# A Hyena filter in the middle of a transformer kernel: decays spread earlier, spectra without the norm, the norm put into the short convolution's weights

## The chip, the cores and the metric

The kernel runs on one core of one Trainium2 chip. The metric is the device time of one execution in microseconds (us). A core has five engines that run their own instruction streams and meet in semaphores: TensorE (PE in the profile; PEld is its weight load), VectorE (DVE), ScalarE (ACT), GpSimd (POOL) and SyncE (SP, which here only issues transfers). SBUF is the on-chip memory of 128 partitions, PSUM holds eight banks of 128 x 512 f32 for the results of matmuls.

## The reference, cut to what matters

The program is a whole model on 512 tokens of width 1024: a first block (a mixer of three attentions, a memory attention, a feed-forward with a convolution), and a second block with four feed-forwards, one pool/Hyena mixer and one latent attention. The change touches the Hyena mixer's filter and what surrounds it:

```python
h = jnp.sin(sin_freq[0] * (z @ w1 + b1))     # three such layers, z: (512, 33), hidden 64
h = (h @ w_out).reshape(L, HYENA_ORDER, 2, HYENA_WIDTH)          # (512, 2, 2, 512)
h = h * jnp.exp(-t[:, None, None, None] * jnp.abs(decay))
fwd, bwd = h[:, :, 0], h[:, :, 1]
two = jnp.concatenate([fwd, zeros, bwd[:0:-1]], axis=0)           # length 1024
two = two * lax.rsqrt(jnp.sum(two * two, axis=0, keepdims=True))
spec = jnp.fft.rfft(two, axis=0)
# in the mixer, for o in 0, 1:
y = irfft(rfft(u, n=2 * L) * spec[o])[:L];  y = y + u * bias[o];  z = parts[o] * y
```

`parts` are the three outputs of a short convolution of width 3 (weights `hyena_conv_w`, bias `hyena_conv_b`) over a projection. The result of the filter does not depend on the tokens.

## The kernel before, in words

**Weights.** All large projections read weights in packs of 128 x 1024 f32 (512 KB). SP loads pack n into one of two raw buffers (L660 to L666) once POOL has split pack n-2. ACT rounds the pack to its high part (`split_high`, L1388), three packs ahead of their use; POOL subtracts to get the low part (`split_low`, L714); PE does three matmuls for each 128 x 128 tile (high x high, high x low, low x high; `pack`, L752, its lines L763 to L765). Four slots of high and low parts are in use. Eight tiles make a pack of a projection, 22 tiles in three packs make one output of a down projection.

**Order of the work.** Each engine has its stream written out by hand. PE: the feed-forward `conv` (L1082), filter layer 1, the feed-forward `ffn0` (L1084), then the filter stage, then the projection `pool_hyena` (16 packs, L1139), then the mixer with its transforms, its out projection and the rest of the second block. In a feed-forward PE does 44 packs up, one small matmul for the filter's hidden layer (`filter_layer`, L1066), and 24 packs down. After pack 0 of the next projection PE sums the squares for the norm (`stats`, L768); ACT takes a root (`root`, L1415), DVE the reciprocal (`norm`, L1983). For each output of a down projection DVE adds the residual and prepares a chunk of the next input (`chunk`, L1965 on DVE, L1401 on ACT). After `conv` the norm is a double one: DVE also accumulates `gained_sq` (L1981, L2354), which the statistics at L775 wait for.

**The filter stage** begins when the last output of `ffn0` has been added to x.
1. ACT issues six transfers on its own queue: the cosine and sine tables (L1759 to L1765), and makes `neg_times` (L1769). PE spreads the four decay rows over the partitions, a matmul of a column of ones with one row each (L1091, banks 4 to 7), and makes the filter of time tile 0 (L1099, banks 0 to 3). ACT takes the absolute value of the spread decays (L1772), then the exponentials for time tile 0 (L1778).
2. For the four time tiles t: DVE multiplies filter and decay (L2369), adds and subtracts the two directions into `fsum` and `fdiff` (L2376, L2377). ACT squares (L1790). PE makes the filters of t+1 and sums the squares of t with a matrix of ones (L1116). In place of filters of a fifth tile PE does the middle row (four matmuls with the alternating signs, L1110).
3. PE makes the spectra in four groups g = (half of the frequencies, order), each eight f32 matmuls into four banks: cosine even, cosine odd, sine even, sine odd (L1134). Group g+2 uses the banks of group g, and waits for `spec_taken`.
4. ACT makes `inv_norm` (Ln, Exp with -0.5, L1799, L1801) and scales the bias row, which a transfer has broadcast to all partitions (L1797, L1803). DVE, for each half group, multiplies even by `inv_norm`, adds the bias to the cosines, multiplies odd by `inv_norm`, adds and subtracts both into `spec` (L2406 to L2413). After groups 0 and 1 it works on the middle row, one partition wide (`middle`, L2388 to L2398).
5. PE starts `pool_hyena` pack 0 when six of the eight half groups are taken (L1138), its statistics wait for all eight (L1143). ACT splits pack 3 (L1807 with j = 0) ahead of this, right after the bias.

Of the kernel before, what the change touches and what calls it, by code (L numbers as in the profile page):

```python
# [26 lines left out]
P = 128  # L27
# [172 lines left out]
def build_program(nc, A, out):  # L200
# [158 lines left out]
    absdecay = put("absdecay", [P, 4 * T])  # L359
# [4 lines left out]
    decay_row = nc.alloc_sbuf_tensor_at("decay_row", [P, T], F32, offset=m3f + 4096)  # L364
# [3 lines left out]
    put, m4n = region(window_at)  # L368
    inv_norm = put("inv_norm", [P, 2, T])
    waves_tmp = put("waves_tmp", [P, 2, T])  # L370
    bias_b = put("bias_b", [P, 2, T])
    assert m4n["at"] <= window_at + 4128 + 2048 + 8192
# [56 lines left out]
    STAT = 7  # L429

# [89 lines left out]
    bias_b_arrived = sem("bias_b_arrived")  # L520
# [16 lines left out]
    norm_read = sem("norm_read")  # L537
    norm_ready = sem("norm_ready")
    bias_scaled = sem("bias_scaled")
# [104 lines left out]
    def _(sp):  # L644
# [22 lines left out]

        load_x(0)
# [76 lines left out]
    def _(pe):  # L745
# [46 lines left out]
        def project_out(phase, rhs, ready, packs_each=1, total=8, order=None):  # L792

            with pe.Fori(0, 2) as i:
                for j in range(4):
                    wait_bank(phase, i, 4, j)
                    for c in range(packs_each):
# [277 lines left out]

        def feed_forward(name, s, hidden_base, layer=None):
            project(name + "_up", 2 * FC, LIN, (chunk_ready, 8 * s), s=s)
            if layer is not None:
                filter_layer(layer)
            project_out(name + "_down", (act_hi, act_lo), (hidden_low, hidden_base), packs_each=3, total=FC)  # L1080
# [6 lines left out]
        pe.wait_ge(wout_arrived, 16 * 6)  # L1087
# [15 lines left out]
        for t in range(QT):  # L1103
            if t + 1 < QT:
                filters(t + 1)
            else:
                pe.wait_ge(fsum_ready, 2)
                for o in range(2):
                    for u in range(2):
                        mm = pe.matmul(ps[0:1, 6 + o, :], col("nyquist"), fsum[:, u, o, :], start=(u == 0), stop=(u == 1))  # L1110
                mm.then_inc(mid_made, 1)
# [10 lines left out]
        for g in range(4):  # L1122
            ft, o = g // 2, g % 2
            cut = slice(ft * P, (ft + 1) * P)
            if g == 1:
                pe.wait_ge(norm_read, 1)
                pe.wait_ge(mid_read, 1)
            for part in range(4):
# [1616 lines left out]
```

## Time and profile before

| what | value |
|---|---|
| median of 3 runs | 2823.34 us (2818.3 to 2825.89) |
| the profiled execution, its own time | 2817.33 us |
| its span, first to last instruction | 2815.3 us |
| PE busy | 2743.7 us, 97% |
| DVE, ACT, POOL busy | 1171.4, 1029.2, 1113.1 us (42%, 37%, 40%) |
| mean granted TensorE clock | 0.995 |
| filter stage in the trace | about 1206 to 1278 us of the span |

Times in the trace are in us from the start of the span. A busy time of PE includes matmuls that overlap in its pipeline, so the spacing of their starts is what one costs. An idle time that the profile shows before an instruction is followed by the instruction of another engine that ended it. An f32 matmul of 512 columns is recorded as two instructions. Lines such as L1981 are lines of the kernel; a row of the timeline merges neighbours of one kind and says with x how many.

### The profile page before, as it was taken

The page shows a single profiled execution, that of the slowest core. Times are in us where ns is not written, and L with a number is a line of the kernel's source. Part 1 is how long each engine was busy: PE and PEld are TensorE (multiplying, and loading weights), DVE is VectorE, ACT ScalarE, POOL GpSimd, SP SyncE. Part 2 cuts the span into 40 slices and gives each one's busy share as a digit, 9 for nine tenths or more (in the row PEclk, how much of TensorE's full clock was granted, in tenths as well). Part 3 has the DMA queues.
Part 4 walks back from the last instruction along what each step waited for, and adds up shares of the span by engine and source line. Part 5 has one row for each costly group of instructions (what it writes and reads, how often), then busy time and mean ns, then how long its engine had stood idle before and what let it go on. Part 6 is the DMA issues. An engine that isn't in the chain of part 4 may idle for free.

```text
span 2815.3 us, 35415 instructions
## 1 busy us (share of the span) xinstructions
PE 2743.7 (97%) x12394; PEld 2174.1 (77%) x12394; DVE 1171.4 (42%) x1912; ACT 1029.2 (37%) x1571; POOL 1113.1 (40%) x473
## 2 busy tenths in 40 slices
PE   8999999999999999989999999999999989999998
PEld 6777777888887888847778888888888744788887
DVE  4886534645434225157873222122221356422212
ACT  4455433444333222242223222232322556323221
POOL 3334433444544444513224444444444420444443
PEclk9999999999999999999999999999999999999999
DMA  5333322333332333322113333333233210233332
GB/s 168 115 97 119 98 75 68 99 91 102 98 111 90 97 97 99 110 68 86 45 38 105 98 96 99 110 94 101 91 101 107 90 45 1 81 99 92 102 99 89
DMA packets 78106, 258.18 MB, mean 92 GB/s; under 512 B 8951, under 2 KB 14583, under 8 KB 77768
## 3 DMA queue, kind: packets, MB, share of 16 engines
q1 hardware_dynamic: 70848, 243.30, 28.3%
q10 hardware_dynamic: 7176, 13.78, 1.5%
q8 instruction: 52, 0.85, 0.1%
q14 instruction: 30, 0.25, 0.0%
HBM read 251.02 MB, written 6.03 MB: 91 GB/s over the span
## 4 chain that ended last, share of the span: by engine, by line
PE 92%; DVE 5%; ACT 1%; issue 1%; DMA 0%; ACTq 0%; DVEq 0%
PE ps L763 27%; PE ps L765 27%; PE ps L764 27%; PE ps L1301 1%; PE ps L1315 1%; PE ps L1329 1%; PE ps L1307 1%; PE ps L1116 1%; PE ps L1048 1%; PE ps L1058 0%; PE ps L981 0%; PE ps L982 0%; PE ps L983 0%; PE ps L883 0%; PE ps L966 0%
## 5 line engine op out<-in xcount | busy, mean ns | idle before, releaser
L716 POOL TENSOR_TENSOR wlo<-raw,whi 128x1024 fp32r<-128x1024 f32 x449 | 1099.1, 2451 | 1656.5 <-ACT whi L1393 1631.5
L763 PE MATMUL ps<-lin_hi,whi 128*128 128x512 f32 x2208 | 867.4, 393 | 6.6 <-DVE waves_tmp L2410 6.6
L765 PE MATMUL ps<-lin_hi,wlo 128*128 128x512 f32 x2208 | 860.2, 390 | 0.0
L764 PE MATMUL ps<-lin_lo,whi 128*128 128x512 f32 x2208 | 860.2, 390 | 0.0
L1393 ACT ACTIVATE whi<-raw 128x1024 fp32r<-128x1024 f32 x452 | 473.5, 1053 | 508.8 <-PE ps L765 443.0
L763 PEld LDWEIGHTS ps<-lin_hi,whi 128*128 128x128 f32 x2208 | 415.2, 188 | 98.9 <-DVE waves_tmp L2410 7.4
L764 PEld LDWEIGHTS ps<-lin_lo,whi 128*128 128x128 f32 x2208 | 415.2, 188 | 88.3 <-issue 2.6
L765 PEld LDWEIGHTS ps<-lin_hi,wlo 128*128 128x128 f32 x2208 | 415.1, 188 | 87.0
L763 PE MATMUL ps<-act_hi,whi 128*128 128x512 f32 x858 | 334.0, 389 | 0.0
L765 PE MATMUL ps<-act_hi,wlo 128*128 128x512 f32 x858 | 333.8, 389 | 0.0
L764 PE MATMUL ps<-act_lo,whi 128*128 128x512 f32 x858 | 333.8, 389 | 0.0
L2048 DVE TENSOR_TENSOR up<-ps,rstd 128x512 f32<-128x512 f32 x88 | 60.8, 691 | 395.4 <-PE ps L765 395.4
L1504 ACT ACTIVATE act_hi<-hidden 128x512 f32 (+1 forms) x88 | 55.6, 632 | 462.5 <-DVE hidden L2071 462.5
L1999 DVE SCALAR_TENSOR_TENSOR x<-ps,x 128x512 f32 x64 | 44.3, 692 | 375.0 <-PE ps L765 374.7
L763 PEld LDWEIGHTS ps<-act_hi,whi 128*128 128x128 f32 x858 | 161.1, 188 | 35.1 <-POOL wlo L716 0.8
L764 PEld LDWEIGHTS ps<-act_lo,whi 128*128 128x128 f32 x858 | 161.1, 188 | 33.6
L765 PEld LDWEIGHTS ps<-act_hi,wlo 128*128 128x128 f32 x858 | 161.1, 188 | 33.1
L2048 DVE TENSOR_TENSOR gate<-ps,rstd 128x512 f32<-128x512 f32 x88 | 60.8, 691 | 188.9 <-PE ps L765 188.2
L1408 ACT ACTIVATE scratch<-x 128x512 f32 x64 | 40.5, 633 | 229.6 <-DVE x L1999 229.6
L763 PE MATMUL ps<-o_hi,whi 128*128 128x512 f32 x256 | 100.5, 392 | 1.7 <-DVE o_lo L2592 1.7
L765 PE MATMUL ps<-o_hi,wlo 128*128 128x512 f32 x256 | 99.6, 389 | 0.0
L764 PE MATMUL ps<-o_lo,whi 128*128 128x512 f32 x256 | 99.6, 389 | 0.0
(374 smaller groups left out, 2704.3 us busy)
## 6 DMA issues: line engine op xcount, KB each, us to landing
raw<-in_packs SPq DMA_DIRECT2D x456, 512.0 KB, 3.6
table<-bias_scratch ACTq DMA_DIRECT2D x12, 256.0 KB, 3.0
bias_scratch<-biasrow ACTq DMA_DIRECT2D x16, 160.0 KB
x<-in_x_t SPq DMA_DIRECT2D x4, 512.0 KB, 8.3
out_t<-x SPq DMA_DIRECT2D x16, 128.0 KB, 1.8
bias_scratch<-biasrow ACTq DMA_DIRECT2D x4, 320.0 KB
mem<-in_mem_t ACTq DMA_DIRECT2D x1, 1024.0 KB, 5.5
pool_count<-in_pool_count ACTq DMA_DIRECT2D x1, 1024.0 KB, 4.9
```

Source lines behind the costliest of these rows:

```text
L716: pool.tensor_tensor(wlo[:, n % 4, :], raw[:, n % 2, :], whi[:, n % 4, :].bitcast(F32), ALU.subtract).then_inc(low_split, 1)
L763: pe.matmul(target, wh, hi[:, k, :], start=(chunk0 + at == 0), stop=False)
L764: pe.matmul(target, wh, lo[:, k, :], start=False, stop=False)
L765: mm = pe.matmul(target, wl, hi[:, k, :], start=False, stop=(chunk0 + at == total - 1))
L1048: mm = pe.matmul(ps[:, att2.banks(u)[0], 0:M], mem_q[:, 2 * h + c, qt * P:(qt + 1) * P], mem_k[:, 2 * h + c, :], start=(c == 0), stop=(c = ...
L1116: pe.matmul(ps[:, 4 + c // 2, :], ones[:, :], filt_sq[t % 2][:, c * T:(c + 1) * T], start=(t == 0 and c % 2 == 0), stop=(t == QT - 1 and c ...
L1301: mm = pe.matmul(ps[:, 2 * p + h, :], q_nope[r:r + 64, 2 * g + p, cut], k_nope[r:r + 64, 2 * g + p, :], start=True, stop=False)
L1393: act.activation(whi[:, n % 4, :], raw[:, n % 2, :], ACT.Copy).then_inc(high_split, 1)
L1408: act.activation(squares[:, d % 2, :], x[:, row, :].rearrange("p a t -> p (a t)"), ACT.Square).then_inc(squares_ready, 1)
L1504: act.activation(act_hi[:, bass.ds(f, 1), :].rearrange("p a t -> p (a t)"), h_buf, ACT.Copy).then_inc(hidden_high, 1)
L1999: dve.scalar_tensor_tensor(out=xc, in0=ps[:, j, :], scalar=factor, in1=xc, op0=ALU.mult, op1=ALU.add).then_inc(outs_done, 1)
L2048: dve.tensor_tensor(target, ps[:, 2 * g + side, :], rstd[:, :], ALU.mult).then_inc(outs_done, 1)
```

## The change

In words: the decay rows are loaded before `ffn0` (into the buffer of the position features, after filter layer 0 has read it), and `neg_times` is made there. The four spreading matmuls run between the up and down halves of `ffn0`, into banks 5, 6, 7 and 2, ACT takes the absolute values there; the third output of the down half waits for them. The six tables are loaded by SP, behind the load of `pool_hyena` pack 4. The middle row's matmuls move from the last square step to after spectrum group 0. The spectra are no longer scaled. The bias becomes an impulse at time 0 of `fsum`: the root of the sum of squares on one partition (ACT, Sqrt) times the bias (one small load), added to one row of `fsum`. The sums of squares, which every partition holds, are brought into columns by eight multiply-and-accumulate instructions with the identity, go through Ln and Exp as 128 x 8, and scale the weights and biases of the short convolution for the two gates. ACT copies each odd spectrum from PSUM, DVE does one add and one subtract for each half group; both middle rows come after group 1. ACT's split of pack 3 of `pool_hyena` comes after the copies.

The pieces follow the file: buffers, SP, PE, ACT, DVE.

```diff
-    absdecay = put("absdecay", [P, 4 * T])
-    decay_row = nc.alloc_sbuf_tensor_at("decay_row", [P, T], F32, offset=m3f + 4096)
+    decay_row = nc.alloc_sbuf_tensor_at("decay_row", [P, T], F32, offset=zpos_at)
+    absdecay = nc.alloc_sbuf_tensor_at("absdecay", [P, 4 * T], F32, offset=m3f + 4096)
+    filter_sums, inv_norm = small[:, 24:32], small[:, 32:40]
+    odd_waves = nc.alloc_sbuf_tensor_at("odd_waves", [P, 2, T], F32, offset=window_at)
+    DECAY_BANKS = (5, 6, 7, 2)
+    WAVE_ORDER = ((1, 0), (1, 1), (0, 1), (0, 0))
...
+        def load_waves():
+            sp.wait_ge(outs_done, OUT_BASE["pool_hyena"])
+            for wave, name in ((cos_f, "dcos"), (sin_f, "dsin")):
+                for half in range(2):
+                    src = A[name].rearrange("(p a) (u h) f -> h p a u f", a=2, h=2)[half][:, :, :, 0:256]
+                    sp.dma_start(wave[64 * half:64 * (half + 1), :, :].rearrange("p (a u) f -> p a u f", a=2), src).then_inc(waves_arrived, 16)
+            for wave, name in ((cos_i, "dcos"), (sin_i, "dsin")):
+                sp.dma_start(wave[:, :, :], A[name][:, 0:2, :]).then_inc(inverse_waves_arrived, 16)
...
             load(n, None)
+            if n == hyena + 4:
+                load_waves()
...
+        def spread_decays():
+            pe.wait_ge(decay_arrived, 16 * 4)
+            pe.wait_ge(final_rooted, 1)
+            pe.wait_ge(root_ready, 4)
+            pe.wait_ge(outs_done, OUT_BASE["ffn0_up"] + 2 * FC - 1)
+            for c in range(4):
+                pe.matmul(ps[:, DECAY_BANKS[c], :], ones[32 * c:32 * c + 1, :], decay_row[32 * c:32 * c + 1, :],
+                          start=True, stop=True).then_inc(decay_spread, 1)
...
-        for c in range(4):
-            pe.matmul(ps[:, 4 + c, :], ones[32 * c:32 * c + 1, :], decay_row[32 * c:32 * c + 1, :], start=True, stop=True).then_inc(decay_spread, 1)
...
             if g == 1:
-                pe.wait_ge(norm_read, 1)
-                pe.wait_ge(mid_read, 1)
+                for n in range(2):
+                    for u in range(2):
+                        mm = pe.matmul(ps[0:1, 6 + n, :], col("nyquist"), fsum[:, u, n, :], start=(u == 0), stop=(u == 1))
+                mm.then_inc(mid_made, 1)
+                pe.wait_ge(filter_steps, 2)
+                pe.wait_ge(roots_made, 1)
+            for at, (sines, odd) in enumerate(WAVE_ORDER):
+                wave, source = ((cos_f, fsum), (sin_f, fdiff))[sines]
+                if g == 1 and at == 2:
+                    pe.wait_ge(mid_read, 1)
+                if g >= 2 and at % 2 == 0:
+                    pe.wait_ge(spec_taken, 2 * (g - 2) + at // 2 + 1)
+                pe.wait_ge((fsum_ready, fdiff_ready)[sines], 2 * odd + 2)
+                for t in (2 * odd + 1, 2 * odd):
+                    if t == 0 and not sines:
+                        pe.wait_ge(filter_steps, 1)
+                    mm = pe.matmul(ps[:, 4 * (g % 2) + at, :], wave[:, t, cut], source[:, t, o, :],
+                                   start=(t % 2 == 1), stop=(t % 2 == 0))
...
+                for c in range(4):
+                    act.wait_ge(decay_spread, c + 1)
+                    act.activation(absdecay[:, c * T:(c + 1) * T], ps[:, DECAY_BANKS[c], :], ACT.Abs).then_inc(abs_ready, 1)
...
         act.wait_ge(times_arrived, 64)
         for half in range(2):
             rows = slice(64 * half, 64 * (half + 1))
             order(act.activation(neg_times[rows, :], time_rows[rows, half::2], ACT.Copy))
+        act.wait_ge(hy_pe, 1)
+        for c in range(4):
+            act.dma_start(decay_row[32 * c:32 * c + 1, :], A["decay"][:, c * T:(c + 1) * T]).then_inc(decay_arrived, 16)
+        feed_forward(1, "ffn0", 3, layer=2)
+        act.wait_ge(outs_done, OUT_BASE["pool_hyena"])
...
-        act.activation(inv_norm[:, :, :], ps[:, 4:6, :], ACT.Ln, scale=float(T * T)).then_inc(norm_read, 1)
-        act.activation(inv_norm[:, :, :], inv_norm[:, :, :], ACT.Exp, scale=-0.5).then_inc(norm_ready, 1)
-        act.activation(bias_b[:, :, :], bias_b[:, :, :], ACT.Copy, scale=1.0 / T).then_inc(bias_scaled, 1)
+        act.activation(root_row[:, :, :], ps[0:1, 4:6, :], ACT.Sqrt).then_inc(roots_made, 1)
+        for g in range(4):
+            for k in range(2):
+                n = 2 * g + k
+                act.wait_ge(spec_made, n + 1)
+                if n >= 2:
+                    act.wait_ge(spec_taken, n - 1)
+                act.activation(odd_waves[:, k, :], ps[:, 4 * (g % 2) + 1 + k, :], ACT.Copy).then_inc(odd_waves_copied, 1)
+            if g == 1:
+                act.wait_ge(filter_steps, 2)
+                order(act.activation(inv_norm, filter_sums, ACT.Ln, scale=float(T * T)))
+                act.activation(inv_norm, inv_norm, ACT.Exp, scale=-0.5).then_inc(norm_ready, 1)
...
+        order(dve.tensor_tensor(root_row[:, :, :], root_row[:, :, :], bias_row[:, :, :], ALU.mult))
+        dve.tensor_tensor(fsum[0:1, 0, :, :], fsum[0:1, 0, :, :], root_row[:, :, :], ALU.add).then_inc(filter_steps, 1)
+        for n in range(8):
+            ins = dve.tensor_tensor_reduce(out=squares[:, 0, 0:P], in0=ps[:, 4 + n // 4, n % 4 * P:(n % 4 + 1) * P], in1=ident[:, :],
+                                           scale=1.0, scalar=0.0, op0=ALU.mult, op1=ALU.add, accum_out=filter_sums[:, n:n + 1])
+            order(ins)
+        dve.sem_inc(filter_steps, 1)
...
-                ins = dve.tensor_tensor(even, ps[:, bank, :], inv_norm[:, o, :], ALU.mult)
-                    dve.tensor_tensor(even, even, bias_b[:, o, :], ALU.add)
-                dve.tensor_tensor(odd, ps[:, bank + 1, :], inv_norm[:, o, :], ALU.mult).then_inc(spec_taken, 1)
-                dve.tensor_tensor(spec[:, o, ft, k, 0, :], even, odd, ALU.add)
-                order(dve.tensor_tensor(spec[:, o, ft, k, 1, :], even, odd, ALU.subtract))
-            if ft == 0:
-                middle(o)
+                dve.wait_ge(odd_waves_copied, n + 1)
+                dve.tensor_tensor(spec[:, o, ft, 1 - k, 0, :], even, odd_waves[:, k, :], ALU.add)
+                dve.tensor_tensor(spec[:, o, ft, 1 - k, 1, :], even, odd_waves[:, k, :], ALU.subtract).then_inc(spec_taken, 1)
+            if g == 0:
+                dve.wait_ge(mid_made, 1)
+                for n in range(2):
+                    ins = dve.tensor_scalar(mid_row[0:1, n, 0, :], ps[0:1, 6 + n, :], 1.0, None, ALU.mult)
+                ins.then_inc(mid_read, 1)
+            elif g == 1:
+                middle(0)
+                middle(1)
+        dve.wait_ge(norm_ready, 1)
+        gains = cols[:, COLS["hyena_w"]:COLS["hyena_w"] + 48].rearrange("p (k a) -> p k a", a=12)[:, :, 0:8]
+        order(dve.tensor_tensor(gains, gains, inv_norm.rearrange("p (k a) -> p k a", k=1).broadcast_to([P, 4, 8]), ALU.mult))
```

## Rows read from the trace of the kernel before

**Rows 1.** The page's part on busy time, engine by engine.

```profile
PE 2743.7 (97%) x12394; PEld 2174.1 (77%) x12394; DVE 1171.4 (42%) x1912; ACT 1029.2 (37%) x1571; POOL 1113.1 (40%) x473
```

**Rows 2.** Timeline of PE: start, us, line, operation, count, idle before.

```profile
1206.96 1.14 PE L1091 MATMUL ps<-decay_row,ones 1*128 1x512 f32 x8 [1.00 <-DVE x L1999]
...
1216.90 4.92 PE L1099 MATMUL ps<-hy_wout,hid 64*128 64x512 f32 x8 [6.87 <-DVE filt L2369]
1221.75 3.70 PE L1116 MATMUL ps<-filt_sq_even,ones 128*128 128x512 f32 x8
...
1236.49 3.59 PE L1110 MATMUL ps<-fsum,cols 128*1 128x512 f32 x8
...
1277.76 0.80 PE L763 MATMUL ps<-lin_hi,whi 128*128 128x512 f32 x1 [6.58 <-DVE waves_tmp L2410]
...
1285.73 1.02 PE L777 MATMUL ps<-sumsq,ones 128*128 128x512 f32 x2
```

**Rows 3.** Stretches: us, busy PE, PEld, DVE, ACT, POOL (instructions), PEclk, DMA share, GB/s.

```profile
1210.00:1217.00 7.00, 0.13 (x3) 0.10 (x1) 0.85 (x2) 5.43 (x10) 0.00 (x0) 0.83 0.97 272
1217.00:1222.00 5.00, 5.00 (x9) 2.15 (x10) 4.65 (x7) 5.00 (x10) 0.00 (x0) 0.55 0.01 3
...
1243.50:1271.00 27.50, 27.50 (x65) 11.97 (x63) 22.66 (x32) 6.54 (x6) 2.35 (x1) 1.00 0.07 20
...
1277.70:1283.00 5.30, 5.24 (x13) 4.14 (x14) 5.13 (x9) 0.00 (x0) 0.00 (x0) 0.51 0.00 0
```

**Rows 4.** Timeline of ACT in the filter stage.

```profile
1207.57 0.63 ACT L1413 ACTIVATE lin_hi<-scratch 128x512 f32 x1
...
1211.95 2.06 ACT L1772 ACTIVATE absdecay<-ps 128x512 f32<-128x512 f32 x4
1214.03 1.28 ACT L1778 ACT_TABLE_LOAD   x1
1215.33 3.17 ACT L1778 ACTIVATE decayed<-absdecay,small 128x512 f32<-128x512 f32 x5
...
1248.00 1.04 ACT L1393 ACTIVATE whi<-raw 128x1024 fp32r<-128x1024 f32 x1
```

**Rows 5.** Timeline of DVE in the filter stage.

```profile
1216.15 1.92 DVE L2369 TENSOR_TENSOR filt<-ps,decayed 128x512 f32<-128x512 f32 x3 [6.53 <-ACT decayed L1778]
...
1234.62 1.22 DVE L2376 TENSOR_TENSOR fsum<-filt 128x1024 f32<-128x1024 f32 x1
...
1252.64 0.69 DVE L2412 TENSOR_TENSOR spec<-waves_tmp 128x512 f32<-128x512 f32 x1
...
1257.33 0.68 DVE L2393 TENSOR_TENSOR mid_row<-spec 1x512 f32<-1x512 f32 x1
...
1261.10 0.68 DVE L2398 TENSOR_SCALAR spec<-spec 1x1024 f32<-1x1024 f32 x1
```

**Rows 6.** Multiply-and-accumulate on 128 x 128, timeline of DVE in the mixer.

```profile
226.45 0.29 DVE L2264 CUSTOM_DVE_ANT_0 pair_probs<-ps,table 128x128 f32<-128x128 f32 x1 [0.61 <-PE ps L966]
226.67 0.08 DVE L2264 DVE_READ_ACCUMULATOR2_ANT small<- 128x1 f32 x1
```

**Rows 7.** A stretch of the down half of ffn0, three packs long.

```profile
1085.97:1100.98 15.01, 15.01 (x67) 12.43 (x67) 13.82 (x13) 3.91 (x5) 4.02 (x2) 1.00 0.19 48
```

**Rows 8.** ACT's queue and POOL in the down half of ffn0.

```profile
1094.21 1.35 ACTq L1474 DMA_DIRECT2D decay_row<-in_decay  x4
...
1096.96 2.40 POOL L716 TENSOR_TENSOR wlo<-raw,whi 128x1024 fp32r<-128x1024 f32 x1 [13.79 <-ACT whi L1393]
```

**Rows 9.** Waits of PE: who ended them, total us, times, longest.

```profile
PE ps L775 <- DVE gained_sq L2354: 1.4, 1, 1.4
```

**Rows 10.** Timeline of ACT, POOL and DVE where conv meets ffn0.

```profile
843.76 1.04 ACT L1393 ACTIVATE whi<-raw 128x1024 fp32r<-128x1024 f32 x1
...
844.88 2.66 POOL L716 TENSOR_TENSOR wlo<-raw,whi 128x1024 fp32r<-128x1024 f32 x1 [4.35 <-ACT whi L1393]
...
845.20 2.88 DVE L1981 TENSOR_TENSOR gained_sq<-gained_sq,gained_squares 128x512 f32<-128x512 f32 x1
```

More of the change, by code:

```diff
@@ L536, in build_program @@
     spec_ready = sem("spec_ready")
[L537 removed]
+    decay_arrived = sem("decay_arrived")
+    roots_made = sem("roots_made")
+    filter_steps = sem("filter_steps")
     norm_ready = sem("norm_ready")
[L539 removed]
+    odd_waves_copied = sem("odd_waves_copied")
     mid_made = sem("mid_made")
@@ L796, in project_out @@
                     wait_bank(phase, i, 4, j)
+                    if taken and taken[0] == j:
+                        pe.wait_ge(*taken[1:])
                     for c in range(packs_each):
@@ L1105, in _ @@
                 filters(t + 1)
[L1106 to L1111, printed above, removed]
             if t == 0:
@@ L1125, in _ @@
             if g == 1:
-                pe.wait_ge(norm_read, 1)
-                pe.wait_ge(mid_read, 1)
-            for part in range(4):
-                wave, source, odd = (cos_f, cos_f, sin_f, sin_f)[part], (fsum, fsum, fdiff, fdiff)[part], part % 2
-                if g >= 2 and odd == 0:
-                    pe.wait_ge(spec_taken, 2 * (g - 2) + part // 2 + 1)
-                pe.wait_ge(fsum_ready if part < 2 else fdiff_ready, 2 * odd + 2)
-                for t in (2 * odd, 2 * odd + 1):
-                    mm = pe.matmul(ps[:, 4 * (g % 2) + part, :], wave[:, t, cut], source[:, t, o, :],
-                                   start=(t % 2 == 0), stop=(t % 2 == 1))
-                if odd:
+                for n in range(2):
[16 more added lines that the diff above has]
+                                   start=(t % 2 == 1), stop=(t % 2 == 0))
+                if at % 2:
                     mm.then_inc(spec_made, 1)
@@ L1472, in load_filter @@
                 act.dma_start(hy_wout[64 * o:64 * o + 64, :], A["fw_out"][:, 2 * o * T:2 * (o + 1) * T]).then_inc(wout_arrived, 16)
-            for c in range(4):
-                act.dma_start(decay_row[32 * c:32 * c + 1, :], A["decay"][:, c * T:(c + 1) * T]).then_inc(wout_arrived, 16)
         def feed_forward(n, name, s, conv=False, layer=None):
@@ L1756, in _ @@
         feed_forward(0, "conv", 2, conv=True, layer=0)
-        feed_forward(1, "ffn0", 3, layer=2)
-        for wave, name in ((cos_f, "dcos"), (sin_f, "dsin")):
-            for half in range(2):
-                src = A[name].rearrange("(p a) (u h) f -> h p a u f", a=2, h=2)[half][:, :, :, 0:256]
-                act.dma_start(wave[64 * half:64 * (half + 1), :, :].rearrange("p (a u) f -> p a u f", a=2), src).then_inc(waves_arrived, 16)
-        for wave, name in ((cos_i, "dcos"), (sin_i, "dsin")):
-            act.dma_start(wave[:, :, :], A[name][:, 0:2, :]).then_inc(inverse_waves_arrived, 16)
         act.wait_ge(times_arrived, 64)
@@ L1769, in _ @@
             order(act.activation(neg_times[rows, :], time_rows[rows, half::2], ACT.Copy))
+        act.wait_ge(hy_pe, 1)
         for c in range(4):
-            act.wait_ge(decay_spread, c + 1)
-            act.activation(absdecay[:, c * T:(c + 1) * T], ps[:, 4 + c, :], ACT.Abs).then_inc(abs_ready, 1)
+            act.dma_start(decay_row[32 * c:32 * c + 1, :], A["decay"][:, c * T:(c + 1) * T]).then_inc(decay_arrived, 16)
+        feed_forward(1, "ffn0", 3, layer=2)
+        act.wait_ge(outs_done, OUT_BASE["pool_hyena"])
         def decay(t, c):
@@ L2379, in _ @@
         dve.wait_ge(filt_squared, 16)
-        dve.wait_ge(norm_ready, 1)
-        dve.wait_ge(mid_made, 1)
-        for o in range(2):
-            ins = dve.tensor_tensor(mid_row[0:1, o, 0, :], ps[0:1, 6 + o, :], inv_norm[0:1, o, :], ALU.mult)
-        ins.then_inc(mid_read, 1)
-        dve.wait_ge(mid_read, 1)
-        dve.wait_ge(bias_scaled, 1)
+        dve.wait_ge(roots_made, 1)
+        dve.wait_ge(bias_row_arrived, 16)
+        order(dve.tensor_tensor(root_row[:, :, :], root_row[:, :, :], bias_row[:, :, :], ALU.mult))
[5 more added lines that the diff above has]
+        dve.sem_inc(filter_steps, 1)
         def middle(o):
```

37 lines of the change are left out of this document (16 added, 21 removed).

## The prediction

> **What bounds the kernel now.** I read the page's busy times first. PE is busy for 97% of the span [rows 1], so only time at which PE stands still, runs slowly, or does work that can go, is worth anything; the reader should ask of each edit whether it touches PE. Then I read PE's timeline through the filter stage [rows 2] beside the granted clock of its stretches [rows 3]. PE ends `ffn0` at 1206, spreads the decays, makes the first filters and stands for 6.87 us until 1216.90. It then works without a gap until 1277.76 - 6.58 = 1271.18, stands for 6.58 us, and starts `pool_hyena` at 1277.76. After each pause the clock is low: 0.55 at 1217 to 1222, 0.51 at 1277.7 to 1283, the level of 1.2 GHz, against 1.00 between [rows 3]. Both pauses end with work of ACT and DVE, so I read those last [rows 4, 5].
>
> **First pause: ACT's queue.** After its last chunk ACT is done at 1207.57 + 0.63 = 1208.20. Six transfer issues and `neg_times` stand between that and Abs at 1211.95; four Abs take 2.06, a table load 1.28, the first exponential starts at 1215.33 and DVE's first product at 1216.15 [rows 4, 5]. After the change the table load follows the chunk: exponential at 1208.2 + 1.3 = 1209.5, first product at 1210.3, 5.8 us sooner. Without the spread PE ends its first filters near 1209 and stands 2 us instead of 6.9, so I expect full clock after it. `filters(1)` is paced by DVE: its last product is then made near 1214.1. Before, the last matmul of it and the start of the squares lie 1.8 us apart at the low clock; at full clock an f32 matmul of 512 columns costs 27.68 / 32 = 0.86 us (1243.5 to 1271.18 holds the 32 of the spectra [rows 2, 3]). Squares start at about 1215.0, not 1221.75.
>
> **Steps to the spectra.** Between 1221.75 and 1236.49 PE does three rounds of squares and two of filters [rows 2]; 3 x 3.43 for the squares leaves about 4.45, 2.2 for each round of filters with its change-over. The fourth squares follow without the middle row: 1215.0 + 14.7 + 3.4 = 1233.1. ACT and DVE need less than PE's 5.6 us for a time tile (the DVE products and the pair of 1.22 each come to 4.9 [rows 5]), so PE sets this. The end was 1236.49 + 3.5 + 3.5 = 1243.5; 10.4 us are gained, 3.4 of them only moved, since the middle row returns after group 0. The tables must be there before ACT's small copy into `sin_f`, after tile 1, now near 1221.6. The stretch 1210 to 1217 moves 272 GB/s at a share of 0.97 [rows 3] and nothing is left at 1217; SP starts them a little sooner than ACT did, behind one weight load that is already in flight. I cost it at nothing; the next load on SP is due only when POOL has split pack 3. ACT's small bias load has two tiles of time.
>
> **Spectra.** PE: 32 + 4 f32 matmuls of 0.86, from 1233.1 to 1264.0. What it waits for on the way, with prices:
> - The impulse: Sqrt of 1 x 1024 like other ACT work of 1024 elements, 1.04 [rows 4]; two DVE steps of 1.22 [rows 5]. Done at 1236.8. Needed by the eighth matmul at 1239.1. Hidden.
> - Eight multiply-and-accumulates of 128 x 128 with a wait each. The mixer's cost 0.29, overlapped to 0.22 from start to start, and 0.08 for the accumulator [rows 6]. Bounds 0.25 and 0.75 (one of 512 columns, 0.69, plus a wait [rows 5]); I take 0.4, which is the row and a wait, 3.2 in all. Done at 1240.0, at worst 1242.8. PE asks after the middle row, at 1243.4. Hidden, by a little at the upper bound.
> - Eight half groups on DVE: two steps of 0.69, 1.35 together, in place of four or five [rows 5]. ACT's copies of 0.63 lie beside PE. Groups 2 and 3 ask for half groups that are over 5 us old.
> - The two middle rows now stand together after group 1. One, without its first step, lasts from 1257.33 to 1261.78 [rows 5], 4.45; two are 9.0 with waits. PE ends group 1 at 1250.3; copy, half group: 1252.4; middles: 1261.4; half groups 4 and 5: 1264.1. That is the wait of `pool_hyena` for six. DVE and PE are level, so any DVE instruction that is dearer shows here one for one.
> - Ln, Exp, two table loads on ACT, 2.8 us, run while DVE does the middles. Hidden. The scaling of 32 values on DVE comes after everything PE needs.
>
> So pack 0 starts at about 1264.2 instead of 1277.76: 13.6 us.
>
> **Clock of pack 0.** From 1277.76 to the statistics at 1285.73 are 7.97 us [rows 2] for 24 matmuls. In `ffn0` 66 matmuls take 15.01 [rows 7], 0.227 each, 5.5 for the pack. Without the pause 2.5 us come back. From the statistics on all is as before relative to PE: the root, the reciprocal and the outputs hang on them. ACT's split of pack 3 moves from 1248.00 [rows 4] to about 1266.7 and POOL's to 1270; PE wants it at 1264.2 + 16.9 = 1281. Cover 11 us. The raw load queued on SP behind POOL comes then, 20 us before PE's pack 5.
>
> **The spread in ffn0.** Eight instructions, 1.07 from start to start of the next [rows 2], between two kinds of matmul on PE that is never idle there: 1.2 us lost, bounds 1.0 and 2.0 (the change-over before it was an idle 1.00 [rows 2]). Its banks were free long before. On ACT four Abs (2.06) replace four issues that took 1.35 and their tail (the next split began 1095.83, 0.27 behind them), so POOL starts 0.5 us after 1096.96 [rows 4, 8] and is done at 1100.1, while PE wants pack 3 at 1101 + 1.2. Hidden, with 2 us of cover; without it it would cost at most 0.5.
>
> **Between conv and ffn0.** ACT gets two small copies and four issues ahead of its split at 843.76 [rows 10]: 0.5 + 1.35 [rows 8] + 0.3, so the split is done near 846.9 and POOL starts there, not at 844.88. That is not only hidden (ACT's root is wanted at 849.7, it is free at 848.2). DVE's step on `gained_sq` lasts 2.88, until 848.08, as long as POOL's split lasts (to 847.54); other such steps take 0.69 [rows 5, 10]. With POOL later it should take 0.69, and PE's only wait here, 1.4 us for `gained_sq` [rows 9], goes. Bounds 0 and 1.4; I take 1.4, because with POOL at 846.9 both DVE steps are over.
>
> **The sum.** 13.6 + 2.5 - 1.2 + 1.4 = 16.3 us. The profiled execution took 2817.33 us by its own time (span 2815.3, 2.0 around it), so 2801.0 in its terms. It lay 6.0 below the median of the runs, 2823.34; against the median the forecast is 2807.0.
>
> **A rule weighed.** The exponential starts at 1215.33, 1.30 behind the start of its table load at 1214.03 [rows 4]: the load's own 1.28 and nothing more. The Trainium skill, ScalarE: Activation LUTs, section "What ACT_TABLE_LOAD costs", gives the load about 1283 ns and adds a drain of about 1380 ns, 2.66 us for every switch. The load of the row agrees, the drain does not show. With such a drain ahead of the load, where ACT has just finished its chunk, the first product would be 1.4 us later and the gain 14.9; I go by the row.
>
> **Rivals.** A measurement of this kernel can tell about 0.3%, 8.5 us, from no change.
> - *The low clock stays in the tile loop.* PE works only in pieces until 1215. For it: the clock was still 0.55 to 1222 after the old pause [rows 3]. Against it: the pause shrinks to 2 us. The first squares would take 3.4 us more, and the filters 1: gain 12, time 2811.
> - *DVE sets the end and a pause remains.* The middles and the half groups are level with PE by my sum. If the eight accumulates push everything past the middle row (0.75 each) and the steps that read PSUM are 0.2 dearer, `pool_hyena` starts 3.5 us later and its clock may fall again, 2.5 more: gain 10, time 2813. For it: the old pause was of this kind. Against it: DVE has half the steps.
> - *The weights or tables come late; slower.* The tables now stand in SP's queue, and ACT's copy into `sin_f` blocks the exponentials behind it. Each us beyond 1221.6 would cost one. To be slower than before the tables would have to land after about 1238, twice the time that they took from 1206.8 to 1217; at 1242 the time would be 2827. For it: rows of 1 KB on the queue that also carries the weights. Against it: the bandwidth of the stretch.
> - *Parts fail to pay*: `gained_sq` is still caught by POOL and the spread costs 2.0: gain 14, inside the forecast's range.
>
> **How the numbers follow.** Forecast 0.74, own range 2802 to 2811. Low clock 0.09, DVE 0.12, slower 0.04, the rest, 0.01, no change. The runs of before spread over 7.6 us, so a median moves by 2 or 3 without a cause: part of the low-gain cases falls within 8.5 us. Faster 0.84, same 0.12, slower 0.04. The range 2800 to 2816 takes in both rivals with a small gain.
>
> **What would show it.** First product of DVE about 3.5 us after PE's last matmul of `ffn0`; no pause of PE over 3 us and a clock near 1.00 to the statistics of `pool_hyena`; squares of tile 3 directly before the spectra; `gained_sq` at 0.69 with no wait at L775; PE's spread 1.1 us. The prediction is wrong if PE waits for the table copy, for the accumulates, or for the half groups by more than 2 us.

## The result, and the profile after

| | kernel before | changed kernel |
|---|---|---|
| median of 5 runs, us | 2822.39 (2818.3 to 2825.89) | 2806.93 (2803.94 to 2812.29) |
| ratio | | 0.9949, interval 0.9934 to 0.9964 |
| profiled execution: own time, span, us | 2817.33, 2815.3 | 2806.62, 2804.6 |

The changed kernel is faster by about 15 us, 0.5%, and the interval of the ratio excludes 1. The two profiled executions differ by 10.7 us only; where the rest is stands below. The page of the changed kernel still has PE as the bound:

```profile
span 2804.6 us, 35427 instructions
PE 2746.8 (98%) x12394; PEld 2175.3 (78%) x12394; DVE 1158.1 (41%) x1909; ACT 1032.5 (37%) x1580; POOL 1112.2 (40%) x473
```

PE's timeline of the changed kernel through the filter stage, to be held against [rows 2] (start, duration, engine, line, operation, count, idle time before and what ended it):

```profile
1207.15 2.00 PE L1128 MATMUL ps<-hy_wout,hid 64*128 64x512 f32 x8 [1.00 <-DVE x L2033]
1211.27 5.14 PE L1128 MATMUL ps<-hy_wout,hid 64*128 64x512 f32 x8 [2.12 <-DVE filt L2403]
1216.34 4.82 PE L1139 MATMUL ps<-filt_sq_even,ones 128*128 128x512 f32 x8
...
1232.10 3.60 PE L1139 MATMUL ps<-filt_sq_odd,ones 128*128 128x512 f32 x8
1235.54 3.60 PE L1165 MATMUL ps<-fdiff,sin_f 128*128 128x512 f32 x8
...
1266.72 0.50 PE L780 MATMUL ps<-lin_hi,whi 128*128 128x512 f32 x1
...
1272.31 1.02 PE L794 MATMUL ps<-sumsq,ones 128*128 128x512 f32 x2
```

The pause of 6.87 us is one of 2.12, the one of 6.58 is gone. Squares of tile 3 stand directly before the spectra. The clock of these stretches and of one in the latent attention (PE, PEld, DVE, ACT, POOL busy with counts, granted clock, DMA share, GB/s), as in [rows 3]:

```profile
1211.20:1216.30 5.10, 5.03 (x8) 1.80 (x8) 4.75 (x8) 5.10 (x10) 0.00 (x0) 0.56 1.01 280
1216.30:1221.00 4.70, 4.70 (x9) 1.93 (x8) 4.67 (x7) 4.18 (x8) 0.00 (x0) 0.75 0.08 29
1221.00:1266.70 45.70, 45.70 (x113) 18.48 (x112) 31.83 (x58) 17.46 (x28) 0.00 (x0) 1.00 0.00 1
1266.70:1272.30 5.60, 5.60 (x25) 4.61 (x25) 4.29 (x5) 2.83 (x3) 2.40 (x1) 1.00 0.06 10
2199.50:2438.00 238.50, 220.43 (x1082) 136.25 (x1082) 123.28 (x231) 136.05 (x292) 54.40 (x37) 0.97 0.15 45
```

The low clock is there again after the short pause, 0.56 and then 0.75; this is what the forecast had excluded. From 1221 on it is full, through pack 0 too, which was at 0.51 before.

I measure the stage from the start of DVE's last residual of `ffn0` (its step on `x` that ends PE's 1.00 of waiting) to the statistics of `pool_hyena`, since whole executions differ by some us before it for other reasons. Before: 1285.73 - 1206.12 = 79.61. Changed: 1272.31 - 1206.31 = 66.00, so 13.6 less. Outside the stage, the spread in `ffn0` costs 1.07 and the stretch between `conv` and `ffn0` is 1.65 shorter (363.28 instead of 364.93 from the statistics of the memory attention to the last ones of `ffn0`, on `gained_sq`). Together 14.2 us, where the medians show 15.5. Of the profiled pair 0.8 is lost in the first mixer, before any edit, and 2.7 in the latent attention, which is not touched: from its statistics to the next ones it lasts 235.49 in the kernel before (2212.93 to 2448.42) and 238.15 here (2199.54 to 2437.69), at a clock of 0.99 and 0.97. The row of the kernel before, to be held against the last one above (whose window is 0.35 wider than the stretch):

```profile
2212.90:2448.40 235.50, 216.95 (x1081) 134.52 (x1080) 123.22 (x231) 135.94 (x292) 54.12 (x37) 0.99 0.15 45
```

### The profile page after: what moved, and what is told of

It is laid out like the page before. It is cut to its first block, busy times and chain, and to the rows that moved or that the text cites. A ratio compares the mean times of both kernels' runs of the same rounds, so it can differ in the third digit from the quotient of the medians.

```text
span 2804.6 us, 35427 instructions
## 1 busy us (share of the span) xinstructions
PE 2746.8 (98%) x12394; PEld 2175.3 (78%) x12394; DVE 1158.1 (41%) x1909; ACT 1032.5 (37%) x1580; POOL 1112.2 (40%) x473
## 4 chain that ended last, share of the span: by engine, by line
PE 94%; DVE 4%; ACT 1%; issue 1%; DMA 0%; DVEq 0%; ACTq 0%
PE ps L780 27%; PE ps L782 27%; PE ps L781 27%; PE ps L1332 1%; PE ps L1346 1%; PE ps L1165 1%; PE ps L1360 1%; PE ps L1338 1%; PE ps L1139 1%; PE ps L1000 1%; PE ps L1067 1%; PE ps L1077 1%; PE ps L1002 0%; PE ps L1001 0%; PE ps L985 0%
```

## The experiments

All kernels with their stage, in us (squares: from the start of the squares of tile 0 to PE's next filters; pause: idle time before pack 0):

| kernel | median (range), us | stage | residual to squares | squares | pause |
|---|---|---|---|---|---|
| before | 2822.4 | 79.61 | 15.63 | 3.63 | 6.58 |
| e11 before again | 2824.9, one run | 82.09 | 15.85 | 6.13 | 6.60 |
| e3 between only | 2821.4, one run | 81.71 | 15.86 | 5.86 | 6.6 |
| e2 new start only | 2816.3 (2814.5 to 2819.7) | 75.88 | 10.02 | 5.87 | 6.60 |
| e1 old start | 2816.5 (2815.1 to 2818.4) | 73.27 | 15.85 | 6.20 | 0 |
| changed | 2806.9 | 66.00 | 10.03 | 4.74 | 0 |
| e8 changed again | 2809.3 (2804.3 to 2812.5) | 67.37 | 10.02 | 6.13 | 0 |
| e4 warm pauses | 2805.1 (2803.8 to 2807.5) | 63.94 | 9.08 | 3.63 | 0 |
| e9 warm again | 2804.4 (2803.9 to 2809.0) | 63.91 | 9.07 | 3.63 | 0 |
| e5 warm all | 2809.1 (2808.2 to 2810.2) | 66.38 | 11.63 | 3.52 | 0 |
| e7 early table | 2805.4 (2801.3 to 2808.7) | 63.11 | 8.25 | 3.64 | 0 |
| e10 DVE late | 2806.5, one run | 65.67 | 9.35 | 3.64 | 1.29 |
| e6 double sums | 2809.0, one run | 64.17 | 9.34 | 3.64 | 0 |

**e1: the change with the old start.** Decays spread after `ffn0`, tables on ACT, Abs before the exponentials; the spectra part of the change stays.

```diff
 # against the changed kernel
-            if n == hyena + 4:
-                load_waves()
 ...
-            if layer == 2:
-                spread_decays()
 ...
+        for c in range(4):
+            pe.matmul(ps[:, 4 + c, :], ones[32 * c:32 * c + 1, :], decay_row[32 * c:32 * c + 1, :], start=True, stop=True).then_inc(decay_spread, 1)
+        # ACT after ffn0: the six table loads, then Abs of banks 4 to 7
```

> The changed kernel with the start of the filter stage as it was: six table transfers and neg_times on ACT, the decays loaded in ffn0's down half, spread and made absolute after ffn0. The measure is the stage from DVE's last residual of ffn0 to the statistics matmul of pool_hyena: 79.6 us in the kernel before, 66.0 in the changed one. My theory (both halves of the change pay separately, and add): the squares of tile 0 start 15.6 us after the last residual as before, not 10.0, and then need 14.7 instead of 15.8 us to the fourth squares because the low clock is over by then: stage 70.6 us, whole kernel 3.5 us slower than the changed one (4.6 less 1.1 of spread). Rival (the two halves overlap, the second hides behind the first): stage above 74 us.

Ratio 0.9976 [0.9966, 0.9985], 7.0 us by the medians (the kernel before beside it: 2823.5). The pause before pack 0 is gone, the one of 6.87 is back. The stage is 2.7 above the expectation, and 2.6 of it are the clock in the squares: 6.20 where the profile of before happened to have 3.63. Missed too was the whole time: 3.5 slower than the changed kernel was expected, the medians (of runs that did not stand beside each other) differ by 9.6, the profiles by 7.3 in the stage and 0.6 outside it.

```profile
1219.94 5.13 PE L1125 MATMUL ps<-hy_wout,hid 64*128 64x512 f32 x8 [6.87 <-DVE filt L2403]
1225.01 6.27 PE L1136 MATMUL ps<-filt_sq_even,ones 128*128 128x512 f32 x8
```

**e2: the kernel before with the new start.** The other half alone: spread, Abs, tables and `neg_times` moved; spectra, norm and bias as before.

```diff
 # against the kernel before
+            if n == hyena + 4:
+                load_waves()
 ...
+            if layer == 2:
+                spread_decays()
+            project_out(name + "_down", (act_hi, act_lo), (hidden_low, hidden_base), packs_each=3, total=FC,
+                        taken=(DECAY_BANKS[3], abs_ready, 4) if layer == 2 else None)
```

> The kernel before with only the new start: decays and neg_times between conv and ffn0, the spread between ffn0's halves, tables loaded by SP; the norm, the bias, the middle row and the spectra as before. My theory: stage 79.6 - 4.6 = 75.0 us, a pause of 6.5 us and the low clock before pool_hyena as before, the wait for gained_sq gone (1.4), spread 1.1: whole kernel 4.9 us faster than before. Rival (PE's first pause is paid back at the second): stage 79 us and no gain beyond 1.4.

Ratio 0.998 [0.997, 0.9989], 7.1 us by the medians, where 4.9 was expected. The start is 5.8 us shorter (15.85 in e11, 10.02 here), the second pause is untouched. The stage, 75.88, is 0.9 above the expectation; its squares had the low clock (5.87). PE's rows of it:

```profile
1213.11 5.13 PE L1124 MATMUL ps<-hy_wout,hid 64*128 64x512 f32 x8 [2.12 <-DVE filt L2390]
1218.17 5.94 PE L1141 MATMUL ps<-filt_sq_even,ones 128*128 128x512 f32 x8
...
1276.44 0.80 PE L776 MATMUL ps<-lin_hi,whi 128*128 128x512 f32 x1 [6.60 <-DVE waves_tmp L2431]
```

The halves add: against e11, whose squares had the same low clock, e1 takes 8.8 off the stage, e2 6.2, the changed kernel in e8 14.7. 8.8 and 6.2 make 15.0. In the medians it is 7.0 and 7.1 against 13.3 to 15.5 for both.

**e4: matmuls in the pauses.** Three f32 matmuls of 512 columns into a bank that nobody reads, one ahead of the first filters (in the 1.00 in which PE waits for the residual), two behind them. If the 2.1 to 3.5 us are lost to the clock, they come back; if the pause itself or DVE costs them, they don't.

```diff
 # against the changed kernel
+        pe.wait_ge(abs_ready, 4)
+        pe.matmul(ps[:, 6, :], ones[:, :], rstd[:, :], start=True, stop=True)
 ...
+        for n in range(2):
+            pe.matmul(ps[:, 6, :], ones[:, :], rstd[:, :], start=True, stop=True)
```

> The changed kernel with three extra f32 matmuls into an unused bank: one before PE waits for the last residual of ffn0, two after the filters of tile 0. They fill the pauses of 1.0 and 2.1 us (0.86 each at full clock). Theory A (the fall of the clock at 1211 comes from these pauses): granted clock near 1.00 throughout, the squares of tile 0 start 1.3 us sooner and run 1.2 us shorter, stage 66.0 - 2.5 = 63.5 us. Theory B (it comes from the thin stretch of filters of tile 1, which DVE paces): clock still falls, stage 66 us or more.

The stage is 63.94, the squares take 3.63. Ratio 0.9942 [0.9925, 0.9958]. **e9** is the same kernel measured again, **e8** the changed kernel again beside it:

> The changed kernel with the two pauses filled by three extra matmuls, beside the changed kernel on the same chip. Theory (pauses make the clock fall): no low clock in the stage, 63.9 us again, and the median 2 to 3 us below the changed kernel's. Rival (the first such run had luck with the clock): stage 66 or more, medians equal.

> The changed kernel once more. My theory: the stage has only one thing that varies, how long the low clock lasts after the first pause; with 6.8 us of it the stage is 66.0 again, with 13.7 (as in the run with the old start) about 68.7. The rest of the kernel varies by low-clock intervals elsewhere (near 230, 1425, 2225 to 2270), so the stage repeats better than the whole. Rival: the gain lies in something else that this trace does not repeat.

e9: 63.91, ratio 0.9941 [0.9928, 0.9955]. e8: 67.37, ratio 0.995 [0.9935, 0.9964]. First e9's rows, then e8's:

```profile
1206.35 1.02 PE L1119 MATMUL ps<-rstd,ones 128*128 128x512 f32 x2
1207.51 2.00 PE L1130 MATMUL ps<-hy_wout,hid 64*128 64x512 f32 x8
1209.43 1.99 PE L1135 MATMUL ps<-rstd,ones 128*128 128x512 f32 x4
1211.62 4.19 PE L1130 MATMUL ps<-hy_wout,hid 64*128 64x512 f32 x8 [0.21 <-DVE filt L2407]
1207.50:1215.70 8.20, 7.80 (x20) 2.69 (x20) 6.25 (x10) 8.11 (x13) 0.00 (x0) 1.00 0.93 255
```

```profile
1213.71 5.13 PE L1128 MATMUL ps<-hy_wout,hid 64*128 64x512 f32 x8 [2.12 <-DVE filt L2403]
1218.77 6.20 PE L1139 MATMUL ps<-filt_sq_even,ones 128*128 128x512 f32 x8
1209.60:1218.80 9.20, 7.08 (x17) 2.79 (x17) 7.26 (x11) 9.12 (x15) 0.00 (x0) 0.72 0.93 271
1213.70:1218.80 5.10, 5.09 (x9) 2.03 (x9) 4.75 (x7) 5.10 (x10) 0.00 (x0) 0.50 0.98 288
1218.80:1224.90 6.10, 6.10 (x9) 2.34 (x8) 5.06 (x7) 5.16 (x10) 0.00 (x0) 0.59 0.02 5
```

Same program but for three matmuls, the same DVE instructions ahead of each step: with the pauses filled the filters of tile 1 take 4.19 and the squares 3.70 at a clock of 1.00; with the pauses left, 5.13 and 6.20 at 0.50 and 0.59. DVE is no later in either: the last product of tile 0 is there 7.96 behind the residual in e4 and 7.97 in the changed kernel. Nor are the transfers: their share is 1.02 over the filters of e4, 1.01 in the changed kernel. So the clock, not DVE, stands between the forecast and the time. By the stage it is worth 2.1 us in the changed profile and 3.5 in e8. It isn't the luck of two traces either: the filters of tile 1 had a full clock in all four kernels with filled pauses (e4, e9, e5, e7), and a low one in all five with the same pauses left: 0.56 in the changed kernel, 0.50 in e8, 0.77 in e2, and 0.61 in e6 and e10, whose squares then had the full clock, so that the stage of e6 (64.17) is only 0.3 above e9's. The rows of e6 and e10:

```profile
1213.80:1218.20 4.40, 4.40 (x9) 1.82 (x9) 4.05 (x7) 4.40 (x9) 0.00 (x0) 0.61 0.95 270
1214.00:1218.40 4.40, 4.40 (x9) 1.82 (x9) 4.05 (x7) 4.40 (x9) 0.00 (x0) 0.61 1.04 284
```

The medians agree in sign (2805.1 and 2804.4 against 2806.9 and 2809.3), but the intervals overlap: that the whole kernel is faster for the extra matmuls is not shown, only that the stage is. Every one of these kernels fills both pauses; which of the two matters, no run tells.

**e5: matmuls between the filters too.** The same and, for each pair of filters of tile 1, one more matmul of 256 columns.

```diff
 # against e4
+                if t == 1:
+                    pe.matmul(ps[:, 6, 0:256], ones[:, :], rstd[:, 0:256], start=True, stop=True)
```

> As the one with the pauses filled, and after each filter matmul of tile 1 another extra f32 matmul of 256 columns (0.43 at full clock). Theory A: clock near 1.00, but PE has 0.9 us of work for each product of DVE and loses up to 0.5 us: stage 64.0. Theory B: this one keeps the clock and the one before does not: stage 64.0 here, 66 there. If the clock falls in both, the extra matmuls cost twice their price and the stage is 68.

Ratio 0.9953 [0.9937, 0.997], the stage 66.38, 2.4 longer than e4's. The clock was already full, so nothing was left to win, and I had priced the matmul at too little (0.43; it takes 0.63). A pair now starts every 1.69 us (e4's four pairs take 4.12 in all, 1.03 each). PE's rows, then DVE's last step on the products of tile 0:

```profile
1215.19 0.70 PE L1133 MATMUL ps<-rstd,ones 128*128 128x256 f32 x2
1215.82 1.13 PE L1130 MATMUL ps<-hy_wout,hid 64*128 64x512 f32 x2
1216.88 0.70 PE L1133 MATMUL ps<-rstd,ones 128*128 128x256 f32 x2
...
1219.20 1.13 PE L1130 MATMUL ps<-hy_wout,hid 64*128 64x512 f32 x2
```

```profile
1216.65 0.48 DVE L2412 MEMSET filt<- 1x512 f32 x1 [0.16 <-DVE filt L2409]
```

The expectation took DVE as what paces PE here, and it isn't: DVE has made all four products by 1217.13, the fourth pair starts only at 1219.20, and DVE itself is not held up (from its first product to the first of tile 1 are 6.06 in e4, 6.07 here). A pair takes 1.06 of PE here and 1.03 in e4, so PE had no room between the pairs, and an extra matmul is paid in full: the squares start 2.55 later (11.63 instead of 9.08).

**e7: the exponential's table early.** With two of the matmuls, an exponential of one column right behind the Abs in `ffn0`, so that the table is loaded there.

```diff
 # against e4
-        for n in range(2):
-            pe.matmul(ps[:, 6, :], ones[:, :], rstd[:, :], start=True, stop=True)
+        pe.matmul(ps[:, 6, :], ones[:, :], rstd[:, :], start=True, stop=True)
 ...
+                act.wait_ge(abs_ready, 4)
+                order(act.activation(small[:, 92:93], absdecay[:, 0:1], ACT.Exp, scale=-1.0))
```

> The pauses filled (one extra matmul instead of two behind the filters of tile 0), and one exponential of a single column on ACT right after the absolute values in ffn0, so that the table for Exp is loaded there and not behind the last chunk. Theory: ACT's squares and copies keep that table, the load of 1.28 us leaves the path, DVE's first product comes when its own sum of squares is done, 0.7 us sooner; stage 63.2. Rival: the table is loaded again at the first exponential of the stage; stage 63.9, or 65 or more if the shorter filling lets the clock fall.

Stage 63.11 (expected 63.2), ratio 0.9939 [0.9925, 0.9952]. ACT's rows of it:

```profile
1097.78 1.28 ACT L1551 ACT_TABLE_LOAD   x1
...
1210.12 0.63 ACT L1447 ACTIVATE lin_hi<-scratch 128x512 f32 x1
1210.65 3.16 ACT L1810 ACTIVATE decayed<-absdecay,small 128x512 f32<-128x512 f32 x5
```

The copies and splits between 1099 and 1210 leave the table as it is, and the exponentials follow the chunk copy directly. The residual to the squares is 8.25 instead of 9.07, so 0.8 of the 1.28 is gained. DVE now does its first product 3.43 behind the residual instead of 4.21, with no idle time before it: its own chunk steps ahead of it are the next limit.

**e10: DVE later at the end.** Two steps of 0.70 between the middle rows and the last half groups, to see whether DVE and PE are level there.

```diff
 # against the changed kernel
+                for n in range(2):
+                    order(dve.tensor_tensor(squares[:, 0, :], x[:, 0, :], x[:, 1, :], ALU.add))
```

> The changed kernel with two more DVE steps of 512 columns (0.69 each, into a scratch buffer) behind the two middle rows. By my sum DVE and PE are level at the start of pool_hyena, so both steps should show one for one: a pause of PE of 1.4 us before pool_hyena and stage + 1.4. Rival (PE alone sets the start, DVE has slack): stage unchanged within 0.3.

```profile
1265.12 1.42 DVE L2454 TENSOR_TENSOR scratch<-x 128x512 f32<-128x512 f32 x2
...
1269.11 0.50 PE L780 MATMUL ps<-lin_hi,whi 128*128 128x512 f32 x1 [1.29 <-DVE spec L2442]
1269.10:1274.70 5.60, 5.59 (x25) 4.62 (x26) 4.11 (x5) 2.83 (x3) 2.39 (x1) 1.00 0.14 16
```

1.4 us more on DVE is a pause of 1.29 on PE: level, with 0.1 to spare. The stage is 65.67, 1.5 above e6's 64.17, which has no such pause and the same time in the squares. The clock stays full after this pause.

**e3: only what moved between `conv` and `ffn0`.** The kernel before with the decay loads and `neg_times` there, spread and spectra as before.

```diff
 # against the kernel before
-            for c in range(4):
-                act.dma_start(decay_row[32 * c:32 * c + 1, :], A["decay"][:, c * T:(c + 1) * T]).then_inc(wout_arrived, 16)
+        # neg_times (moved here), then after hy_pe:
+        for c in range(4):
+            act.dma_start(decay_row[32 * c:32 * c + 1, :], A["decay"][:, c * T:(c + 1) * T]).then_inc(wout_arrived, 16)
```

> The kernel before with only this: neg_times and the four decay loads are issued between conv and ffn0, ahead of ACT's split of pack 3. Theory (POOL's split and DVE's step on gained_sq hinder each other): POOL's split starts 2 us later, the step takes 0.69 instead of 2.88, PE has no wait at L775, 1.4 us less from conv's last residual to the statistics. The first pause of the filter stage shrinks by 0.5 (neg_times gone), stage 79.1 with the same low clock. Rival (POOL catches the next DVE step instead): the wait stays at 1 us or more.

**e11** is the kernel before once more, to see whether the wait of [rows 9] is always there:

> The kernel before once more, for a second look at its stage and at its low-clock intervals. Theory: stage 79.6 if the low clock after the first pause ends before the first squares, up to 83 if it reaches over them; the pause of 6.6 before pool_hyena is there in either case, and the 2.88 of gained_sq too. Rival: the stage of before varies for another reason than its low-clock intervals.

e11's waits, then e3's DVE and ACT at the place:

```profile
PE ps L775 <- DVE gained_sq L2354: 1.4, 1, 1.4
```

```profile
845.37 1.14 ACTq L1761 DMA_DIRECT2D decay_row<-in_decay  x4
...
846.36 0.68 DVE L1982 TENSOR_TENSOR gained_sq<-gained_sq,gained_squares 128x512 f32<-128x512 f32 x1
846.62 1.06 ACT L1393 ACTIVATE whi<-raw 128x1024 fp32r<-128x1024 f32 x1 [1.27 <-issue]
```

In e11 the step on `gained_sq` lasts 2.88 again and PE waits 1.41; in e3 it lasts 0.68, is over at 847.04, POOL's split starts only at 847.75, and PE does not wait. From the statistics of the memory attention to the last ones of `ffn0` are 363.29 in e3 and 364.93 in the kernel before. Four transfer issues and two small copies that delay ACT remove a wait of PE.

The rest of e3's expectation missed. Its stage is 81.71, not 79.1: 2.2 of that is the low clock in the squares (5.86 instead of 3.63), and the 0.5 for `neg_times` did not come. The first product stands 10.06 behind the residual, 10.03 in the kernel before, because ACT's issues for the sine table took 1.80 instead of 1.30. Its whole time, 2821.4 against 2822.8 of the kernel before beside it, is one run of each and tells nothing. e11 kept its expectation: stage 82.09 with the low clock reaching over the squares (6.13), the pause of 6.60 there.

**e6: the eight accumulates twice.**

```diff
 # against the changed kernel
+        for n in range(8):
+            ins = dve.tensor_tensor_reduce(out=squares[:, 0, 0:P], in0=ps[:, 4 + n // 4, n % 4 * P:(n % 4 + 1) * P], in1=ident[:, :],
+                                           scale=1.0, scalar=0.0, op0=ALU.mult, op1=ALU.add, accum_out=filter_sums[:, n:n + 1])
+            order(ins)
```

> The changed kernel with the eight multiply-and-accumulates done twice. They take 2.8 us and end at 35.7 us into the stage; PE asks for them 39.7 into it. Theory (hidden behind the middle row): DVE is 2.8 us later up to the middle row's read and level again at the third half group; no pause of PE, stage 64.0 to 67.4, by the low clock of the run alone (63.9 with none, 64.4 with 3.4 us of it, 66.0 with 6.8, 67.4 with 10.2). Rival (the delay is carried along on DVE to the start of pool_hyena, which is level): a pause of 2.8 us there and 2.8 more.

```profile
1267.46 0.50 PE L780 MATMUL ps<-lin_hi,whi 128*128 128x512 f32 x1
```

PE's first row of pack 0 has no idle time before it, and DVE's second eight end at 1245.4: the sums could cost twice as much and stay hidden. PE asks for them at 1246.76, so 1.4 us of cover are left even so. The stage of 64.17 lies in the expected 64.0 to 67.4.

## Why the prediction was right, and which step of it failed

The forecast was 2807.0 and the median is 2806.9, but that agreement is closer than its steps, and in part luck. The forecast gain of 16.3 stands against 13.3 to 15.5 in medians and 14.2 in the profiles, and it was taken from a median of before of 2823.3; the five runs beside the changed kernel gave 2822.4. One step was wrong by about 2 us, and differences of that size come and go between medians of one and the same kernel (2806.9, and 2809.3 in e8). Where the gain comes from was forecast rightly.

- **First pause, right but for its consequence.** DVE's first product comes 1210.52 - 1206.31 = 4.21 behind the residual, instead of 10.03: 5.8 sooner, as worked out. The exponential starts 1.30 behind its table load, as in [rows 4]; the drain that the Trainium skill adds (ScalarE: Activation LUTs, "What ACT_TABLE_LOAD costs") doesn't show here either. ACT's rows of the changed kernel:

```profile
1208.40 1.28 ACT L1805 ACT_TABLE_LOAD   x1
1209.70 2.56 ACT L1805 ACTIVATE decayed<-absdecay,small 128x512 f32<-128x512 f32 x4
```

- **The step that failed:** "PE ends its first filters near 1209 and stands 2 us instead of 6.9, so I expect full clock after it." PE stood 2.12 us, and the clock was 0.56 over the filters of tile 1 and 0.75 in the squares: 5.07 from the first of these filters to the squares where a full clock gives 4.12 (e4), and 4.74 for the squares where it gives 3.63. Counted from the residual, the squares start 1.15 later than forecast (10.03 against 1215.0 - 1206.12 = 8.88) and take 1.1 longer. This was the first rival, at a chance of 0.09. Its mechanism came true and its price of 4.3 was too high for this profile (2.1 by the stage against e4 and e9) and near it in e8 (3.5). I had looked at the second pause alone. Before it stand 1.00 of waiting and the filters of tile 0, 2.00 for eight instructions that use 64 rows; with both gaps filled, the clock is 1.00. Whether the first gap and these filters have a share in the fall, no run shows, since none filled one gap alone. With this step right, the stage would have been 79.61 - 13.6 - 2.5 = 63.5; e9 measured 63.91.
- **Steps to the spectra and the spectra, right.** From the end of the squares of tile 0, 1221.08, to pack 0, 1266.72, are 45.6; the forecast had 1215.0 + 3.5 to 1264.1, also 45.6. The accumulates stand 0.33 apart, 2.7 in all (forecast 3.2, from 0.4 each), done before PE asks, and e6 shows the cover. That DVE and PE are level at pack 0 was right within 0.1, by these rows of the changed kernel (the last step that PE waits for, ending at 1266.66) and by e10:

```profile
1239.34 0.27 DVE L2419 CUSTOM_DVE_ANT_0 scratch<-ps,ident 128x128 f32<-128x128 f32 x1
...
1239.65 0.29 DVE L2419 CUSTOM_DVE_ANT_0 scratch<-ps,ident 128x128 f32<-128x128 f32 x1
...
1265.98 0.68 DVE L2442 TENSOR_TENSOR spec<-ps,odd_waves 128x512 f32<-128x512 f32 x1
```

- **Two smaller slips of the working.** The sign "first product of DVE about 3.5 us after PE's last matmul" doesn't fit its own sum, 1210.3 against an end of `ffn0` at 1206, which makes 4.3; measured are 4.4. And tables that land at 1238 would have taken three times as long as those of the kernel before (1206.8 to 1217), not twice. Of the other signs, the clock near 1.00 up to the statistics failed, the rest came.
- **Clock of pack 0, right.** 1266.72 to 1272.31 is 5.59, against 7.97 before: 2.4, forecast 2.5.
- **The spread, right:** 1.07 from start to start, forecast 1.2. The tables were never waited for.

```profile
1085.11 1.14 PE L1101 MATMUL ps<-decay_row,ones 1*128 1x512 f32 x8
1086.18 0.50 PE L780 MATMUL ps<-act_hi,whi 128*128 128x512 f32 x1
```

- **`gained_sq`, right.** The changed kernel's DVE step takes 0.69, POOL's split comes behind it, and the wait of [rows 9] is gone; the stretch is 1.65 shorter where 1.4 was forecast. e3 and e11 show it apart from the rest of the change.

```profile
845.98 0.69 DVE L2015 TENSOR_TENSOR gained_sq<-gained_sq,gained_squares 128x512 f32<-128x512 f32 x1
...
847.37 2.42 POOL L733 TENSOR_TENSOR wlo<-raw,whi 128x1024 fp32r<-128x1024 f32 x1 [6.07 <-ACT whi L1424]
```

What stays open: which of the two gaps makes the clock fall; why the squares had the full clock in some executions (before, e10, e6) and not in others (e11, e3, e8) behind the same or nearly the same pauses; and what starts the stretches of low clock in the first mixer and the latent attention, which make whole executions differ by up to 3 us at places that no edit touches.

The best of these kernels is that of e4 and e9 (2805.1 and 2804.4), with e7's beside it (2805.4 and the shortest stage, 63.11); between them and the changed kernel the whole times don't decide, the stages do.

## What to carry to other kernels

A short pause of PE isn't priced by its own length: look at the clock behind it, and at other waits and small matmuls close to it. Where other engines make PE wait anyway, a few matmuls into a free bank cost nothing here and kept the clock. Put them only where PE stands idle; where its own work stands in a row, each is paid in full. To see a gain of a few us in a kernel this long, compare a stage of the trace, from one event of the same kind to another, besides the whole times.

## What the runs showed of the hardware

- Pauses of 1.00 and 2.12 with 2.00 of 64-row f32 matmuls between them were followed by a granted clock of 0.56 and 0.75 (0.50 and 0.59 in e8), that is partly or wholly 1.2 GHz; three f32 matmuls in them kept 1.00, 2.4 GHz (e4, e9; in e7, two). Over the first filters and the 2.12 themselves the clock was still 1.00 (1207.1 to 1211.2): it fell when PE was at work again. After the pause of 1.29 in e10 the clock stayed at 1.00.
- After the same pause of 6.87 the squares took 3.63 once and 6.13 to 6.20 twice (before; e11 and e1). One execution says what such a stretch can cost, not what it costs.
- A DVE step with two SBUF inputs is slowed beside POOL's split: 0.69 becomes 2.88 [rows 10], and the scaling of 128 x 32 takes 2.02 while POOL's split runs from 1268.55 to 1270.95, and ends with it at 1270.99 (in e10 it starts 0.17 later in the split, takes 1.85 and again ends with it; no trace has this step without a split beside it). The Trainium skill, GPSIMD Engine Reference, section "1. Specifications", says that the two engines share SBUF interfaces and that VectorE instructions with two SBUF inputs contend; these rows agree.

```profile
1268.55 2.40 POOL L733 TENSOR_TENSOR wlo<-raw,whi 128x1024 fp32r<-128x1024 f32 x1 [62.90 <-ACT whi L1424]
1268.97 2.02 DVE L2455 TENSOR_TENSOR cols<-cols,small 128x32 f32<-128x32 f32 x1
```
